# The down projection of two of four blocks as seven products of half-size matrices

## The chip, the cores and the metric

One core of one Trainium2 chip runs the whole step. The metric is the device time of one execution in microseconds, given as the median of some runs; the profile is of one execution.

## The reference, cut to what matters

One layer of a streaming encoder on 2048 prompt frames and 32 frames of a running stream. All is float32.

```python
m = g[:, :, 0] * attn + g[:, :, 1] * conv
x = x + rmsnorm(m @ w_out, g_post_mix)
h = rmsnorm(x, g_pre_ffn)
f = (silu(h @ w_ffn_gate) * (h @ w_ffn_up)) @ w_ffn_down    # 1024 -> 2816 -> 1024
return x + rmsnorm(f, g_post_ffn)
```

The change touches the product with `w_ffn_down`: for 512 frames a matrix of 512 x 2816 times one of 2816 x 1024.

## The kernel before, in words

**Tiling.** The prompt is worked off in four blocks of 512 frames (`NB`, `T`); the last takes the 32 sample frames along (`ext(b)`). A block is a list of 80 steps (`KINDS`): 50 of input projection, attention and convolution, 8 of `w_out`, and 22 of `w_ffn_down` (from `S_D`); the gate and up stage stands between the last two. Each float32 product is made of three: an operand is split into a high part (rounded to fp32r, by ACT) and a low part (operand minus high part, by DVE), and PE computes high x high, high x low and low x high into one PSUM bank.

**Gate and up** (`gate_and_up`, L1406). Pairs of 2 x 2 half-size matrices are multiplied with seven products instead of eight, 146 slots (`SLOTS`), 12 matmuls of 256 columns a product. The weights come as raw tiles or, from block 1 on, as stored sums of tiles, and are split on chip by `high_weights` (ACT, L1792) and `low_weights` (DVE, L2422), up to five units ahead of PE (`AHEAD`). In block 0 POOL forms the sums (`summed_weights`, L1161). The outputs f, 22 tiles of 128 features by 512 frames, are written by `copies_out` (ACT, L1841) and `products_out` (DVE, L2450; L2481 is its last multiplication).

**Down** (`token_major`, L1451, and `down_tail`, L1492). A step takes two tiles of f (256 features) and half of the output columns. `staged_hi` (L1825) and `staged_lo` (L2431) split f two tiles at a time, one step ahead. The weights, split in block 0 and stored in DRAM, come back as high and low tiles of 512 KB by `load_hi` and `load_lo` (L984, L997). For each of four frame tiles (128 frames) and each of the two feature tiles PE makes three matmuls of 512 columns (L1447 to L1449): the piece of f is the stationary operand, the weight streams. The results stand in all eight PSUM banks; the first two banks are copied out at half-time (`stash`).

**Beside the down stage** the next block's input norm is made, tile by tile in fixed steps (`s0_at`, L769): SP loads x (`load_x`), ACT sums squares (`sum_squares`, L1744), POOL takes the root (`inv_rms`, L1150), DVE scales (`scale_rows`, L2345), PE transposes (`transpose_tile`, L1289), DVE multiplies by the gains (`gains_in`, L2354), ACT rounds (`normed_hi`, L1786), DVE subtracts (`normed_lo`, L2363). After the last step each of four output tiles gets its root mean square (`post_squares`, `post_inv_rms`) and is added to x (`residual`, L2483); then SP stores y (`store_y`, L1047), and the next block's first convolution taps wait for that store.

**Order.** Every engine has its own queue, written out by hand, and works it off in order; semaphores (`w_used`: PE has used a step; `fhi_ok`, `flo_ok`: a piece of f is split; `hf_ok`, `hlo_ok`: a norm tile is made) tie them together. A wait in a queue holds all that stands behind it.

## Time and profile before

| | us |
|---|---|
| median of 3 runs | 2989.41 (2988.89 to 2991.73) |
| the profiled execution | 2988.57 |
| its span | 2986.8 |
| granted clock of TensorE, mean | 0.997 of 2.4 GHz |
| PE busy, share of the span | 98% |

The page gives, for one execution, the busy time of each engine (PE is TensorE, DVE VectorE, ACT ScalarE, POOL GpSimd, SP the engine that issues most DMAs), groups of instructions with their mean duration and what ended the idle time before them, and the DMAs. Matmuls overlap in their pipeline: their pace is read from start to start, not from the duration. The same holds, to a smaller degree, for ACT and DVE.

### The profile page before, as it was taken

How to read it: one execution, taken by the hardware profiler on the slowest of the kernel's cores; microseconds unless marked ns; L12 is line 12 of the kernel's file. 1: busy time of each engine (PE TensorE's matmuls, PEld its weight loads, DVE VectorE, ACT ScalarE, POOL GpSimd, SP SyncE). 2: the span in 40 equal slices, each digit the busy share in tenths (PEclk: the TensorE clock that was granted, in tenths of full speed). 3: DMA queues.
4: the chain of work that ended last, by engine and by line, in shares of the span. 5: the costliest groups of instructions: out<-in, count | busy, mean ns of one | idle time of the engine just before them, and what ended most of it. 6: DMA issues, size and time to landing. Idle time of an engine off the chain costs nothing. (4 is left out here: it accounts for less than half of the span.)

```text
span 2986.8 us, 50911 instructions
## 1 busy us (share of the span) xinstructions
PE 2932.4 (98%) x18791; PEld 2618.2 (88%) x18791; DVE 2030.7 (68%) x3674; ACT 1451.5 (49%) x2877; POOL 680.0 (23%) x658
## 2 busy tenths in 40 slices
PE   8999999999999999999999999999999999999998
PEld 7777789988888889998888888999899999899976
DVE  8998779874797747663398775665369867466623
ACT  5766555554455535553155544554225554455412
POOL 4950035520581000000086000000039400100001
PEclk9999999999999999999999999999999999999999
DMA  8875746678654355556655444556565443445543
GB/s 297 274 244 200 268 146 210 206 280 300 223 190 166 128 187 166 179 182 226 218 195 185 142 156 158 188 186 210 196 208 173 169 132 121 170 157 172 178 168 122
DMA packets 204454, 573.44 MB, mean 192 GB/s; under 512 B 24000, under 2 KB 26816, under 8 KB 203696
## 3 DMA queue, kind: packets, MB, share of 16 engines
q1 hardware_dynamic: 191728, 548.81, 54.2%
q10 hardware_dynamic: 12480, 21.38, 1.9%
q8 instruction: 151, 2.47, 0.3%
q14 instruction: 95, 0.78, 0.1%
HBM read 456.03 MB, written 114.16 MB: 191 GB/s over the span
## 5 line engine op out<-in xcount | busy, mean ns | idle before, releaser
L1325 PE MATMUL PS<-h_hi,w_hi 128*128 128x512 f32 (+2 forms) x1664 | 533.4, 353 | 9.0 <-DVE u L2710 5.4
L1325 PE MATMUL PS<-h_hi,w_lo 128*128 128x512 f32 (+2 forms) x1664 | 525.3, 349 | 0.0
L1325 PE MATMUL PS<-h_lo,w_hi 128*128 128x512 f32 (+2 forms) x1664 | 525.3, 348 | 0.0
L1355 PE MATMUL PS<-op_hi,w_hi 128*128 128x256 f32 x1680 | 476.6, 284 | 2.2 <-DVE w_lo L2429 2.2
L1355 PE MATMUL PS<-op_lo,w_hi 128*128 128x256 f32 x1680 | 475.4, 283 | 0.0
L1355 PE MATMUL PS<-op_hi,w_lo 128*128 128x256 f32 x1680 | 475.4, 283 | 0.0
L1221 POOL TENSOR_TENSOR y<-y,prod 128x512 f32<-128x512 f32 (+1 forms) x333 | 431.8, 1325 | 157.9 <-ACT prod L1947 144.9
L2314 DVE SCALAR_TENSOR_TENSOR PS<-u,dw,PS 128x512 f32<-128x512 f32 (+1 forms) x604 | 434.1, 766 | 7.0
L2429 DVE TENSOR_TENSOR w_lo<-raw,w_hi 128x512 fp32r<-128x512 f32 x376 | 287.8, 775 | 155.1 <-ACT w_hi L1799 154.3
L1325 PEld LDWEIGHTS PS<-h_hi,w_hi 128*128 128x128 f32 x1664 | 293.9, 188 | 53.3 <-issue 13.1
L1325 PEld LDWEIGHTS PS<-h_hi,w_lo 128*128 128x128 f32 x1664 | 294.0, 188 | 39.3
L1325 PEld LDWEIGHTS PS<-h_lo,w_hi 128*128 128x128 f32 x1664 | 294.3, 188 | 38.5 <-issue 1.4
L1355 PEld LDWEIGHTS PS<-op_hi,w_hi 128*128 128x128 f32 x1680 | 322.4, 192 | 4.0 <-DVE w_lo L2429 3.9
L1355 PEld LDWEIGHTS PS<-op_lo,w_hi 128*128 128x128 f32 x1680 | 322.5, 192 | 0.0
L1355 PEld LDWEIGHTS PS<-op_hi,w_lo 128*128 128x128 f32 x1680 | 322.5, 192 | 0.0
L1192 POOL TENSOR_TENSOR prs<-pss 128x1 f32<-128x1 f32 x34 | 9.3, 274 | 1315.8 <-ACT tmp L1899 1315.8
L1447 PE MATMUL PS<-w_hi,f_hi 128*128 128x512 f32 x704 | 275.4, 391 | 2.0 <-DVE f_lo L2439 1.3
L1947 ACT ACTIVATE prod<-u,dw 128x512 f32<-128x512 f32 (+1 forms) x333 | 234.7, 732 | 83.1 <-POOL y L1221 82.8
L1449 PE MATMUL PS<-w_hi,f_lo 128*128 128x512 f32 x704 | 274.4, 390 | 0.0
L1448 PE MATMUL PS<-w_lo,f_hi 128*128 128x512 f32 x704 | 274.4, 390 | 0.0
L1799 ACT ACTIVATE w_hi<-raw 128x512 fp32r<-128x512 f32 x376 | 225.2, 622 | 50.9 <-POOL raw L1184 50.9
L1833 ACT ACTIVATE f_hi<-f 128x1024 fp32r<-128x1024 f32 (+1 forms) x88 | 94.3, 1072 | 279.6 <-PE PS L1449 177.1
(316 smaller groups left out, 5864.0 us busy)
## 6 DMA issues: line engine op xcount, KB each, us to landing
w_lo<-lo_dram SPq DMA_DIRECT2D x240, 512.0 KB, 4.5
w_hi<-hi_dram SPq DMA_DIRECT2D x240, 512.0 KB, 3.6
raw<-in_w_stream SPq DMA_DIRECT2D x292, 256.0 KB, 3.4
w_raw<-sum_dram SPq DMA_DIRECT2D x180, 256.0 KB, 3.0
w_raw<-in_w_stream SPq DMA_DIRECT2D x80, 512.0 KB, 5.2
hi_dram<-w_hi SPq DMA_DIRECT2D x80, 512.0 KB, 5.6
lo_dram<-w_lo SPq DMA_DIRECT2D x80, 512.0 KB, 3.7
sum_dram<-raw ACTq DMA_DIRECT2D x60, 256.0 KB, 2.3
```

Of the source, the lines that this page charges most:

```text
L1192: link(nc.gpsimd.tensor_tensor(prs[:, c, :], pss[:, tt, 0:1], pss[:, tt, 1:2], ALU.add))
L1221: nc.gpsimd.tensor_tensor(y[:, ct, 0:yw], y[:, ct, 0:yw], prod[:, n % RING, 0:yw], ALU.add).then_inc(prod_used, 1)
L1325: last = nc.tensor.matmul(PS[:, k0 + off, col:col + n], w, x[:, k, c0:c0 + n], start=first and k == 0, stop=stop and k == KT - 1)
L1355: last = nc.tensor.matmul(out, w[:, part_k], o[:, k, :], start=start and first and k == 0, stop=stop and k == KH - 1, skip_group_check=again)
L1447: nc.tensor.matmul(out, hi, wk[0], start=first, stop=False)
L1448: nc.tensor.matmul(out, hi, wk[1], start=False, stop=False)
L1449: return nc.tensor.matmul(out, lo, wk[0], start=False, stop=last_k)
L1799: A(product_hi(m), source(b, m), ACT.Copy).then_inc(wh_ok, 1)
L1833: A(f_hi[:, dd % 2, :, 0:c], f[:, 2 * kp:2 * kp + 2, 0:c], ACT.Copy).then_inc(fhi_ok, 1)
L1947: A(prod[:, n % RING, 0:yw], u[:, ct, k:k + yw], ACT.Copy, scale=dw[:, ct, k:k + 1]).then_inc(prod_ok, 1)
L2314: ins = STT(out, src, dw[:, ct, k:k + 1], acc(b, ct), ALU.mult, ALU.add)
L2429: TT(product_lo(m), source(b, m), product_hi(m).bitcast(F32), ALU.subtract).then_inc(wl_ok, 1)
```

## The change

In blocks 1 and 2 (`SEVEN`) the down product is cut into a 2 x 2 scheme too: first and second half of the frames, even and odd tiles of f, first and second half of the output columns. Seven products, each of 256 frames by 11 tiles of 128 features by 512 columns, take the place of eight. A piece is one product's one feature tile: 77 pieces (`DOWN`), and in each two frame tiles and three matmuls, six matmuls of 512 columns of the same kind as before.

- The factors that are sums or differences of pieces of f are formed on POOL in place (`sum_of_pieces`, 44 of the 77 pieces), nine pieces ahead as its queue is written. ACT and DVE split each piece's factor, 128 x 256 (`high_piece`, `low_piece`), five pieces ahead, in a ring of six.
- The weights are no longer read back split: all seven come as raw tiles of 128 x 512 and are split by ACT and DVE in each of the two blocks. Products 1, 2 and 3 read the weight as it is; 4 to 7 read sums, which POOL forms during block 1's gate and up stage (`sums_of_weights`: 88 sums, 66 DMAs issued by POOL) and stores in `t_dram`. The room for this, `t_sum`, lies over f's last three tiles and a part of x's buffer, so ACT waits for the last store before it writes f's tile 19, and SP before it loads x.
- The products are combined by one copy each of ACT behind products 1, 6 and 7 (`hold`) and five additions of 128 x 1024 on DVE.
- The norm steps of the next block hang on pieces (`STEP_END`: step dd ends with piece 3, 6, 10, 13, 17, 20, 24, 27, 31 ...), and its PSUM pair is the same two banks for all four tiles, so a tile's squares wait for the gains of the one before.
- Squares and residuals of output tiles 0 and 1 move to pieces 70 and 74; those of tiles 2 and 3 stay at the end.

```diff
+SEVEN = (1, 2)
+MAKES_T = SEVEN[0]
+KEPT = ()
+X2, Z2, Y2, W2 = 2, 4, 6, 0
+def passes():
+    order = []
+    for lead, other in ((1, 5), (2, 6), (4, 7)):
+        order += [(lead, 0), (lead, 1)]
+        for e in range(HALF_D - 2):
+            order += [(lead, e + 2), (other, e)]
+        order += [(other, HALF_D - 2), (other, HALF_D - 1)]
+    return order + [(3, e) for e in range(HALF_D)]
+DOWN = passes()
+ND7 = len(DOWN)
+DSLOT = {ie: n for n, ie in enumerate(DOWN)}
+PLACE = [v % 7 if v < 49 else (v - 49) % 8 for v in range(ND7)]
+FR = 6
+DAHEAD = 5
+SUM_AHEAD = 9
+SUMS_F = [(i, e) for i in (5, 6, 7, 3) for e in range(HALF_D)]
+SUM_POS = {ie: n for n, ie in enumerate(SUMS_F)}
+STEP_END = [-(-7 * (dd + 1) // 2) - 1 for dd in range(FT)]
+W_USED_AT = {v: v - 1 for v in range(1, 18)} | {71: 17, 73: 18, 74: 19, 75: 20}
...
+        d_hi = at("d_hi", R_u, [P, FR, 2 * P], F32R)
+        d_lo = at("d_lo", R_u + FR * 2 * P * 4, [P, FR, 2 * P], F32R)
+        held = at("held", R_u + 2 * FR * 2 * P * 4, [P, 2, T])
+        third = at("third", R_u + 2 * FR * 2 * P * 4 + 2 * T * 4, [P, 2, T])
...
+        t_sum = at("t_sum", R_g + (FT - 3) * TX * 4, [P, 2, 2, 2, T // 2])
...
+        t_dram = nc.dram_tensor("t_dram", [HALF_D, 2, P, 2, 2, T // 2], F32, kind="Internal").ap()
...
+        def loaded_later(g):
+            return g >= NS and not (seven(g // NS) and g % NS >= S_D)
...
+        def turned_before(eng, b, tt):
+            if b and seven(b - 1):
+                if tt:
+                    eng.wait_ge(hf_ok, first_norm(b, tt))
+            elif b and tt >= 2:
+                eng.wait_ge(hf_ok, first_norm(b, tt) - 1)
...
+        def place_free(eng, b, v):
+            before = [u for u in range(v) if PLACE[u] == PLACE[v]]
+            if before:
+                down_used(eng, b, before[-1])
+            else:
+                unit_used(eng, b, NU - 8 + PLACE[v])
...
+            def down_units(b):
+                k = 0
+                for v, (i, e) in enumerate(DOWN):
+                    place_free(sp, b, v)
...
+                    elif i < 4:
+                        s = S_D + 2 * FT + e + (HALF_D if i == 3 else 0)
+                        cols_of = slice(0, HW) if i == 1 else slice(HW, 2 * HW)
+                        sp.dma_start(down_raw(v), w_stream[s, :, cols_of]).then_inc(rawq_in[PLACE[v]], 16)
+                    else:
+                        half, odd = {5: (0, 0), 4: (0, 1), 7: (1, 0), 6: (1, 1)}[i]
+                        sp.dma_start(down_raw(v).rearrange("p (c n) -> p c n", c=2),
+                                     t_dram[e, :, :, half, odd, :].rearrange("c p n -> p c n")
+                                     ).then_inc(rawq_in[PLACE[v]], 16)
+                    for dd in steps_at(v - DAHEAD):
+                        if dd % 2 and (dd + 1) // 2 < tiles(b + 1):
+                            load_x(b + 1, (dd + 1) // 2)
...
+            def sums_of_weights():
+                pool.wait_ge(op_ok, len(OPS) * (MAKES_T + 1))
+                made = len(SUMS) * NP
+                for e in range(HALF_D):
+                    for n in range(2):
+                        if e == 0:
+                            load_of_sums(e, n)
+                        elif n == 0:
+                            load_of_sums(e, 0)
+                            load_of_sums(e, 1)
+                    for n in range(2):
+                        b11, b21, b12, b22 = (t_sum[:, n, half, odd, :] for half in range(2) for odd in range(2))
+                        pool.wait_ge(t_in[n], 32 * (e + 1))
+                        nc.gpsimd.tensor_tensor(b11, b12, b11, ALU.subtract).then_inc(ws_ok, 1)
+                        pool.wait_ge(ws_ok, made + 1)
+                        nc.gpsimd.tensor_tensor(b12, b22, b12, ALU.subtract).then_inc(ws_ok, 1)
+                        pool.wait_ge(ws_ok, made + 2)
+                        nc.gpsimd.tensor_tensor(b22, b22, b11, ALU.subtract).then_inc(ws_ok, 1)
+                        pool.wait_ge(ws_ok, made + 3)
+                        nc.gpsimd.tensor_tensor(b21, b21, b22, ALU.subtract).then_inc(ws_ok, 1)
+                        made += 4
+                        pool.wait_ge(ws_ok, made)
+                        pool.dma_start(t_dram[e, n], t_sum[:, n]).then_inc(t_out[n], 16)
+            def load_of_sums(e, n):
+                if e:
+                    pool.wait_ge(t_out[n], 16 * e)
+                cols_of = slice(n * T // 2, (n + 1) * T // 2)
+                for half in range(2):
+                    src = w_stream[S_D + 2 * FT + half * HALF_D + e].rearrange("p (k n) -> p k n", k=2)
+                    pool.dma_start(t_sum[:, n, half], src[:, :, cols_of]).then_inc(t_in[n], 16)
...
+            def sum_of_pieces(b, i, e):
+                a11, a12, a21, a22 = first_half(e, 0), first_half(e, 1), second_half(e, 0), second_half(e, 1)
+                if i == 5:
+                    up_out(pool, b, e)
+                    out, one, other, op = a21, a21, a22, ALU.add
+                elif i == 6:
+                    low_piece_made(pool, b, DSLOT[1, e])
+                    sum_made(pool, b, (5, e))
+                    out, one, other, op = a11, a21, a11, ALU.subtract
+                elif i == 7:
+                    low_piece_made(pool, b, DSLOT[5, e])
+                    sum_made(pool, b, (6, e))
+                    out, one, other, op = a21, a22, a11, ALU.subtract
+                else:
+                    low_piece_made(pool, b, DSLOT[2, e])
+                    sum_made(pool, b, (6, e))
+                    out, one, other, op = a12, a12, a11, ALU.subtract
+                nc.gpsimd.tensor_tensor(out, one, other, op).then_inc(ws_ok, 1)
+            def sums_for(b, first, end):
+                for v in range(first, min(end, ND7)):
+                    if DOWN[v] in SUM_POS:
+                        sum_of_pieces(b, *DOWN[v])
...
+                        if b == MAKES_T:
+                            sums_of_weights()
+                    if s == S_D and seven(b):
+                        sums_for(b, 0, SUM_AHEAD)
+                        for v in range(ND7):
+                            sums_for(b, v + SUM_AHEAD, v + SUM_AHEAD + 1)
+                            for dd in steps_at(v):
+                                start, _, _ = s0_at(S_D + dd, b)
+                                if start is not None:
+                                    inv_rms(b + 1, start, 0)
...
+            def down_of_seven(b):
+                for v, (i, e) in enumerate(DOWN):
+                    if i in KEPT:
+                        down_landed(pe, b, v)
+                    else:
+                        pe.wait_ge(weight_low_ok, 1 + raw_units(b, v))
+                    low_piece_made(pe, b, v)
+                    k = {1: X2, 6: X2, 7: X2, 5: Z2, 2: Y2, 3: Y2, 4: W2}[i]
+                    if e == 0:
+                        if i in (1, 5, 2):
+                            for bank in (k, k + 1):
+                                out_made(pe, b, *last_read(bank))
+                        elif i == 4:
+                            pe.wait_ge(hf_ok, first_norm(b + 1, tiles(b + 1) - 1) + 1)
+                        elif i == 3:
+                            combined(pe, b, 1)
+                        else:
+                            pe.wait_ge(copies_ok, 1 + 3 * sevens_before(b) + (1 if i == 6 else 2))
+                    hi, lo = down_high(v), down_low(v)
+                    for t in range(2):
+                        x_hi, x_lo = (d[:, v % FR, t * P:(t + 1) * P] for d in (d_hi, d_lo))
+                        for x, w, start, stop in ((x_hi, hi, True, False), (x_hi, lo, False, False),
+                                                  (x_lo, hi, False, True)):
+                            last = nc.tensor.matmul(PS[:, k + t, :], x, w, start=start and e == 0 and i not in (6, 7),
+                                                    stop=stop and e == HALF_D - 1, skip_group_check=i in (6, 7))
+                        if t == 0 and v in W_USED_AT:
+                            last.then_inc(w_used, 1)
+                    last.then_inc(w_used if v == ND7 - 1 else dm_used, 1)
+                    for dd in steps_at(v):
+                        _, trans, _ = s0_at(S_D + dd, b)
+                        if trans is not None:
+                            transpose_tile(b + 1, trans, 0)
...
+            def high_piece(b, v):
+                if v >= ND7:
+                    return
+                i, e = DOWN[v]
+                if v < FR:
+                    finished(act, b, (FT - 1, 2))
+                else:
+                    down_used(act, b, v - FR)
+                if (i, e) in SUM_POS:
+                    sum_made(act, b, (i, e))
+                elif i in (1, 4):
+                    up_out(act, b, e)
+                A(d_hi[:, v % FR, :], f_piece(v), ACT.Copy).then_inc(fhi_ok, 1)
+                if i not in KEPT:
+                    down_landed(act, b, v)
+                    place_free(act, b, v)
+                    A(down_high(v), down_raw(v), ACT.Copy).then_inc(weight_high_ok, 1)
+            def hold(b, v):
+                down_used(act, b, v)
+                if DOWN[v][0] == 1:
+                    out = stash_of(b, 1)
+                else:
+                    out = held[:] if DOWN[v][0] == 6 else third[:]
+                    finished(act, b, (FT - 1, 4))
+                A(out, two_banks(X2), ACT.Copy).then_inc(copies_ok, 1)
+            def down_of_seven(b):
+                for v, (i, e) in enumerate(DOWN):
+                    high_piece(b, v + DAHEAD)
+                    if i in (1, 6, 7) and e == HALF_D - 1:
+                        hold(b, v)
+                    for dd in steps_at(v):
+                        start, _, out = s0_at(S_D + dd, b)
+                        if out is not None:
+                            normed_hi(b + 1, out)
+                        if start is not None:
+                            sum_squares(b + 1, start, 0)
+                    if v == DSLOT[3, 4]:
+                        combined(act, b, 4)
+                        first_squares(b, 1)
+                        post_squares(b, 0, 1)
+                        post_squares(b, 1, 1)
...
+                    if b == MAKES_T and j == FT - 3:
+                        for n in range(2):
+                            act.wait_ge(t_out[n], 16 * HALF_D)
...
+                            if LAST_SLOT - 7 <= slot < LAST_SLOT - 7 + DAHEAD and seven(b):
+                                high_piece(b, slot - LAST_SLOT + 7)
...
+                if seven(b):
+                    combined(act, b, 5)
+                    post_squares(b, 2, 1)
+                    post_squares(b, 3, 1)
...
+            def low_piece(b, v):
+                if v >= ND7:
+                    return
+                dve.wait_ge(fhi_ok, pieces_before(b) + v + 1)
+                TT(d_lo[:, v % FR, :], f_piece(v), d_hi[:, v % FR, :].bitcast(F32), ALU.subtract).then_inc(flo_ok, 1)
+                if DOWN[v][0] not in KEPT:
+                    dve.wait_ge(weight_high_ok, 1 + raw_units(b, v))
+                    TT(down_low(v), down_raw(v), down_high(v).bitcast(F32), ALU.subtract).then_inc(weight_low_ok, 1)
+            def down_of_seven(b):
+                for v, (i, e) in enumerate(DOWN):
+                    low_piece(b, v + DAHEAD)
+                    if e == HALF_D - 1:
+                        if i == 2:
+                            down_used(dve, b, v)
+                            dve.wait_ge(copies_ok, 1 + 3 * sevens_before(b) + 1)
+                            TT(stash_of(b, 1), two_banks(Y2), stash_of(b, 1), ALU.add).then_inc(c_ok, 1)
+                        elif i == 6:
+                            dve.wait_ge(copies_ok, 1 + 3 * sevens_before(b) + 2)
+                            TT(held[:], two_banks(Z2), held[:], ALU.add).then_inc(c_ok, 1)
+                        elif i == 7:
+                            dve.wait_ge(copies_ok, 1 + 3 * sevens_before(b) + 3)
+                            combined(dve, b, 2)
+                            TT(two_banks(Z2), two_banks(Z2), third[:], ALU.add).then_inc(c_ok, 1)
+                            combined(dve, b, 3)
+                            TT(third[:], two_banks(W2), third[:], ALU.add).then_inc(c_ok, 1)
+                        elif i == 3:
+                            down_used(dve, b, v)
+                            TT(held[:], two_banks(Y2), held[:], ALU.add).then_inc(c_ok, 1)
+                    for dd in steps_at(v):
+                        start, _, out = s0_at(S_D + dd, b)
+                        if out is not None:
+                            gains_in(b + 1, out)
+                        if start is not None:
+                            scale_rows(b + 1, start)
+                        if out is not None:
+                            normed_lo(b + 1, out)
+                    if v == DSLOT[3, 8]:
+                        residual(b, 0, 1)
+                        residual(b, 1, 1)
...
+                            if LAST_SLOT - 6 <= slot < LAST_SLOT - 6 + DAHEAD and seven(b):
+                                low_piece(b, slot - LAST_SLOT + 6)
...
-                for tt in range(4):
+                for tt in range(2 if seven(b) else 0, 4):
...
```

Not shown: counts of semaphores that follow from the new number of pieces, and four semaphores renamed.

## Rows read from the trace of the kernel before

**Rows 1.** The page: its span, and busy time of the engines.

```profile
span 2986.8 us, 50911 instructions
...
PE 2932.4 (98%) x18791; PEld 2618.2 (88%) x18791; DVE 2030.7 (68%) x3674; ACT 1451.5 (49%) x2877; POOL 680.0 (23%) x658
```

**Rows 2.** Windows: stretch, us, busy PE, PEld, DVE, ACT, POOL, clock, DMA share, GB/s.

```profile
390.00:626.00 236.00, 230.33 (x1872) 227.28 (x1872) 201.91 (x265) 127.49 (x269) 119.65 (x92) 0.99 0.54 185
1106.00:1341.00 235.00, 233.08 (x1903) 230.64 (x1902) 157.23 (x267) 130.64 (x274) 5.74 (x17) 1.00 0.52 164
1346.50:1470.00 123.50, 123.50 (x562) 102.38 (x561) 43.21 (x46) 36.09 (x49) 6.46 (x17) 1.00 0.59 202
```

**Rows 3.** Timeline, PE, block 1 down stage; columns: start us, us, instruction.

```profile
1346.54 0.40 PE L1447 MATMUL PS<-w_hi,f_hi 128*128 128x512 f32 x1
...
1357.22 0.39 PE L1449 MATMUL PS<-w_hi,f_lo 128*128 128x512 f32 x1
...
1357.45 1.03 PE L1302 MATMUL PS<-ident_sb,xs 128*128 128x128 f32 x8
...
1470.01 0.39 PE L1325 MATMUL PS<-h_hi,w_hi 128*128 128x512 f32 x1
```

**Rows 4.** Timeline of block 0 gate and up stage: DVE, then ACT.

```profile
499.89 0.41 DVE L2463 TENSOR_TENSOR part<-PS,part 128x256 f32<-128x256 f32 x1
...
500.22 0.68 DVE L2429 TENSOR_TENSOR w_lo<-s_sum,w_hi 128x512 fp32r<-128x512 f32 x1
...
500.82 0.41 DVE L2457 TENSOR_TENSOR f<-PS,f 128x256 f32<-128x256 f32 x1
...
502.25 0.62 ACT L1799 ACTIVATE w_hi<-raw 128x512 fp32r<-128x512 f32 x1
...
502.77 0.41 ACT L1856 ACTIVATE f<-f 128x256 f32<-128x256 f32 x1
```

**Rows 5.** The page, DMA issues; last column: median us from issue to landing.

```profile
w_lo<-lo_dram SPq DMA_DIRECT2D x240, 512.0 KB, 4.5
...
raw<-in_w_stream SPq DMA_DIRECT2D x292, 256.0 KB, 3.4
```

**Rows 6.** Timeline, DVE, norms of the next block in block 1 down stage.

```profile
1360.01 1.28 DVE L2360 TENSOR_TENSOR xs<-PS,gn 128x512 f32<-128x512 f32 x2
...
1364.37 0.75 DVE L2350 TENSOR_SCALAR xs<-xs,stats 128x1024 f32<-128x1024 f32 x1 [3.08 <-POOL stats L1158]
...
1366.18 1.22 DVE L2439 TENSOR_TENSOR f_lo<-f,f_hi 128x1024 fp32r<-128x1024 f32 x1
...
1397.74 1.22 DVE L2366 TENSOR_TENSOR h_lo<-xs,h_hi 128x1024 fp32r<-128x1024 f32 x1 [1.13 <-ACT h_hi L1789]
```

**Rows 7.** Block 0 against block 1 for L2481; timeline of a clash; POOL sum L1230.

```profile
L2481 DVE TENSOR_TENSOR f<-f,part x18: 1506/1510/1515, 445.0 to 618.6; 128x256 f32<-128x256 f32 x18
...
L2481 DVE TENSOR_TENSOR f<-f,part x19: 415/419/420, 1160.8 to 1341.4; 128x256 f32<-128x256 f32 x19
...
504.07 1.56 POOL L1184 TENSOR_TENSOR raw<-raw,raw 128x512 f32<-128x512 f32 x1
...
504.74 1.44 DVE L2429 TENSOR_TENSOR w_lo<-raw,w_hi 128x512 fp32r<-128x512 f32 x1
...
L1230 POOL TENSOR_TENSOR sq_sum<-y x4: 1286/1295/1432, 181.8 to 2337.0; 128x512 f32<-128x512 f32 x3, 128x574 f32<-128x574 f32 x1
```

**Rows 8.** Waits of PE in block 0; last operand and tile 19 of block 1.

```profile
PE PS L1355 <- DVE w_lo L2429: 2.2, 4, 1.4
...
1149.19 1.23 DVE L2418 TENSOR_TENSOR op_lo<-h,op_hi 128x1024 fp32r<-128x1024 f32 x1
...
1313.62 0.38 ACT L1847 ACTIVATE f<-PS 128x256 f32<-128x256 f32 x1 [0.54 <-PE PS L1355]
```

**Rows 9.** Timeline, DVE then PE, mean of y in block 2.

```profile
1615.06 0.69 DVE L2328 TENSOR_TENSOR sq_sum<-sq_sum,rest_sum 128x512 f32<-128x512 f32 x1
...
1618.85 1.02 PE L1616 MATMUL PS<-sq_sum,ones 128*128 128x512 f32 x2
```

156 lines of the change are left out of this document (123 added, 33 removed).

## The prediction

> **What bounds the kernel now.** I read the page's table of engines, then windows by stage, then the timelines. The page: PE is busy for 98% of the span, DVE for 68% [rows 1]. The windows: in block 1's gate and up stage PE is busy 233 of 235 us and DVE 157; in its down stage PE 123.5 of 123.5 and DVE 43 [rows 2]. So a down stage lasts as long as its matmuls, and fewer of them shorten it as long as the others can feed PE at the new pace. The median of the runs, 2989.4, lies 0.8 above the profiled execution's 2988.6, whose span is 2986.8; I add differences to the median. About 0.2% (6 us) is what can be told from no change.
>
> **What goes.** A matmul of 512 columns is shown as 0.39 us long, but the next starts 0.227 us later (1357.22 to 1357.45) [rows 3]. A stage has 22 steps x 4 token tiles x 2 x 3 = 528 of them, 119.7 us. It runs from 1346.54 to 1470.01, 123.5 us; the other 3.8 are four groups of eight transposes with the seams around them, 0.95 a group. Afterwards a stage has 77 pieces x 2 x 3 = 462 matmuls, 104.7 us (1.36 a piece), and with the 3.8 108.5. Alone that is 15.0 a stage, 30.0 in two.
>
> **What each piece costs the others.** Counted from start to start, DVE takes 0.60 us for 512 columns and 0.33 for 256; ACT takes 0.52 for 512 and at most 0.41 for 256 [rows 4]. DVE now makes the low half of a factor (256) and of a weight (512): 0.93 us a piece; ACT 0.93 at most. Both are under 1.36. The first five pieces are made in the last slots of the gate and up stage, where DVE waits on PE anyway. The weights' DMAs (256 KB each 1.36 us, 193 GB/s, against 202 now [rows 2]) delay nothing of themselves, since a place is refilled seven pieces ahead (9.5 us) and a load lands in 3.4 [rows 5]. But they set where DVE is: the weight of piece v+5 is asked for when v-2 is done and lands 3.5 later, then come ACT (0.55) and DVE (0.7), so DVE reaches what stands behind low_piece(v+5) some 3.4 us after PE starts v.
>
> **The norms of the next block** stand in DVE's queue there. One in the middle runs so now [rows 6]: gains_in at 1360.01, ACT's copy and squares, POOL's root, scale_rows at 1364.37, normed_lo, next instruction at 1366.18. That is 6.17 us of DVE's queue, 3.08 of it waiting, and 5.1 to the scaled tile. The last has no scaling: 1.28 + 1.13 of waiting + 1.22 = 3.6. In the new order they stand at pieces 10, 17, 24 and 31, and PE's transposes of the tile scaled at 10 stand behind piece 13, 5.4 us after the start of 10. The tile is ready at 3.4 + 5.1 = 8.5: PE waits 3.1. From norm to norm DVE needs 6.17 + 7 x 0.93 = 12.7; round the loop (5.1 to the tile, 0.95, three pieces 4.1, 3.4 to the next norm) it is 13.5. PE's own work is 10.5.
>
> **POOL's sums** are the term that decides. 44 of the 77 pieces need a sum on POOL, of two SBUF tensors of 256 columns. Where POOL adds, DVE instructions with two SBUF inputs stand still: L2481 (256 columns) takes 1510 ns in block 0, all 18 times, and 419 in block 1; in the timeline a w_lo issued under a POOL sum ends 0.55 after it, and that sum itself is 0.27 longer than its usual 1.29 [rows 7]. Both DVE instructions of a piece have two SBUF inputs. POOL needs 1.29 for 512 columns and 1.43 for 574 [rows 7], so for 256 about 0.72, an estimate. Of POOL's 1.29 DVE lost 1.09; of 0.72 it then loses 0.52. The ends: nothing (the sums fall into DVE's waits) and the whole 0.72. I take 0.52, since DVE has no slack where the sums lie. POOL's queue is tied to the pieces only through inv_rms: after 10 it makes three sums, after 17 four, and after 24 nothing holds it, so the last 28 come as fast as it can make them, two a piece, some 25 of them under DVE's work.
>
> The Trainium skill (GPSIMD Engine Reference, Specifications) says the same of the SBUF interfaces: "contention with DVE instructions in a 2-port perf mode or with two SBUF inputs"; the trace agrees with it (1510 ns against 419). The same page (Instruction dispatch) gives about 2.5 cycles an element for a two-input loop, at its 1.2 GHz 0.53 us for 256 columns; by that estimate a sum costs DVE 0.33, and two stages come out 12 us shorter than below. For 512 columns it would give 1.07 where the rows have 1.29, so the rows stand.
>
> **One stage**, from the start of piece 10 to that of 42: 3.4, then 12.7 + 3 x 0.52 = 14.3, then 12.7 + 4 x 0.52 = 14.8, then 6.17 + 13 x 0.93 + 3.6 + 25 x 0.52 = 34.9; together 67.4. PE alone needs 32 x 1.36 + 3 x 0.95 = 46.4 and so stands 21.0. The stage takes 108.5 + 21.0 = 129.5 instead of 123.5: 6.0 more, 12.0 in two. Behind 42 DVE (0.93) is faster than PE again and no sums are left; the additions that combine the products wait for PE with five pieces (6.8 us) in hand, and ACT's `hold` copies have the same cover.
>
> **Block 1's gate and up stage** gets 88 sums and 66 DMAs on POOL. (a) DVE goes from 157 us busy to 157 + 88 x 0.52 = 203 of 235, what block 0 has (202), and there PE waited 2.2 for w_lo [rows 2, 8]. I take 2; ends 0 and 5. (b) No DMA issued by POOL is in the trace. A round has two transfers one behind the other (3.5 each, by the nearest rows [rows 5]) and eight sums with their gaps (6.8), each 0.27 late behind DVE as in [rows 7] (2.2): 16.0, eleven rounds 176. The last operand is made at 1150.4, and ACT writes f's tile 19 at 1313.6 [rows 8], 163 later. Its wait then holds ACT 13 us; weights are split five ahead (7 us), so PE stands 6. Ends: 0 (rounds under 14.8) and 30 (rounds of 18.2). The Trainium skill (DMA: Bandwidth & Descriptors, Specifications) has about 1 us to the first byte for DMAs issued by GpSimd against 0.6 for the others; that would add 0.8 a round, 9 in all, to (b), and no run here shows it. SP waits for the same stores before the next x and the first piece, hidden if ACT's wait is.
>
> **Elsewhere.** (c) load_x(2) holds SP until the first normed_lo; the load of piece 19 comes about 3 us late, inside the 14.3. (d) Two of four tiles' squares and residuals move into the stage. The other two come behind an addition of 1.2; the last residual ends some 8.6 after the last matmul, now 5.8, and the store of y, and the first tap after it, as much later. y's mean is ready at 1615.75 and PE uses it at 1618.85 [rows 9]: 3.1 of cover for 2.8. 0; without cover up to 3 a boundary. (e) `w_used` opens the next block's first weights 4.5 pieces (6.1 us) before the end; a 512 KB load lands in 4.5 [rows 5]. 0; ends 0 and 2.
>
> Total: 2989.4 + 12.0 + 2 + 6 = 3009.
>
> **Rivals.**
> *No clash, the norms bind (faster).* POOL's sums fall where DVE waits. From 10 to 42: 3.4 + 13.5 + 13.5 + 25.1 (5.1 + 0.95 + 14 x 1.36) = 55.5; PE stands 9.1, stage 117.6, two save 11.8: 2978. It decides if a sum costs DVE less than about 0.2. For it: block 0's 80 sums cost DVE 45 us (202 against 157), 0.56 each for twice the columns, and PE 2 [rows 2, 8]. Against: there DVE had slack and read PSUM often. 0.15.
> *All hidden.* The lead of five pieces covers norms and sums: 2989.4 - 30.0 = 2959. The place of the transposes speaks against it. 0.07.
> *Half a clash.* 0.3 a sum: 32 x 0.22 = 7.0 less a stage: 2989.4 - 2.0 + 3 = 2990. 0.13.
> *Whole sums lost, or late stores.* 0.72: 32 x 0.20 = 6.4 more a stage, 3009 + 13 = 3022; or (b) at its end, 3009 + 24 = 3033. 0.20.
> *It doesn't do what it says*: that PE's count does not fall is excluded by the loops, 77 x 6 against 528.
> Forecast 0.45, from 2997 to 3018.
>
> **How the numbers follow.** Faster by over 0.2%: 0.15 + 0.07 = 0.22. Within: 0.13. Slower: 0.45 + 0.20 = 0.65. The range leaves out the hidden case (0.07) and the upper half of the late stores: 2972 to 3028.
>
> **What would show it.** Pieces 1.36 apart until 10; PE waiting on DVE's xs before the second to fourth group of transposes, 2 to 4 us each; w_lo stretched to 1.2 us, with PE waiting on it, between pieces 28 and 42, under 28 POOL sums in a row; then none; stages of 129. In block 1, ACT waiting for a store of t_dram at tile 19. Wrong if w_lo keeps its 0.69 there, if PE's waits sit behind 42 (then a DMA or `hold`), or if POOL's sums of weights are done long before 1313.

## The result, and the profile after

The changed kernel takes 3044.9 us (3041.9 to 3048.6, 4 runs) against 2990.6 (2988.9 to 2994.4, 4 runs): ratio 1.018, interval 1.0163 to 1.0198. It is 54 us slower where 20 were forecast, above the forecast's 2997 to 3018 and above the wider range's 3028. The profiled execution is the slowest of the four (3048.6); its span is 60.0 us longer than that of the profiled execution before, and the places below are counted in it.

The page, as in [rows 1]:

```profile
span 3046.8 us, 51830 instructions
...
PE 2925.1 (96%) x18659; PEld 2606.4 (86%) x18659; DVE 2189.2 (72%) x3948; ACT 1547.6 (51%) x3143; POOL 899.5 (30%) x900
```

The windows of block 1's gate and up stage, the part of it in which POOL works, and the two down stages, as in [rows 2] (busy time of PE, PEld, DVE, ACT, POOL, then clock, DMA share, GB/s):

```profile
1119.00:1375.30 256.30, 229.66 (x1890) 229.09 (x1890) 176.41 (x273) 129.11 (x274) 129.83 (x164) 0.95 0.74 245
1150.00:1316.00 166.00, 166.00 (x1386) 166.00 (x1385) 128.80 (x199) 91.55 (x200) 106.51 (x128) 1.00 0.90 301
...
1375.30:1510.60 135.30, 117.69 (x497) 94.25 (x496) 110.66 (x174) 80.43 (x172) 46.23 (x53) 0.94 0.53 162
2102.30:2238.10 135.80, 116.80 (x504) 93.87 (x503) 110.87 (x178) 82.26 (x175) 49.87 (x55) 0.96 0.53 162
```

PE has less to do than before and still the span is longer. From first matmul to first matmul, in us:

| part | before | after | more |
|---|---|---|---|
| start to block 1's gate and up | 1119.0 | 1120.3 | 1.3 |
| block 1's gate and up | 227.5 | 255.0 | 27.5 |
| its down stage | 123.5 | 135.3 | 11.8 |
| to block 2's gate and up | 362.6 | 364.2 | 1.6 |
| block 2's gate and up | 227.6 | 227.5 | -0.1 |
| its down stage | 124.4 | 135.8 | 11.4 |
| to block 3's gate and up | 407.3 | 412.7 | 5.4 |
| the rest | 395.0 | 396.0 | 1.0 |

Who made PE wait, over the whole span (us in total, times, longest):

```profile
PE PS L1564 <- DVE xs L2712: 26.5, 7, 5.7
PE PS L1617 <- ACT f L2198: 24.7, 1, 24.7
PE PS L1798 <- DVE w_lo L2812: 10.1, 12, 4.1
...
PE PS L1587 <- DVE x L2916: 5.2, 1, 5.2
```

None of the four stood before. Each row is read: who waited, for whose result, us in total, times, longest. L1564 are the transposes of the next norm and `xs` the scaled tile that they take; L1617 are the gate and up products, L1798 the seven down products with `w_lo` the low half of their weight, L1587 block 3's first steps.

**The wait at tile 19.** From the timelines, one round of POOL, and ACT behind the last store (start us, us, instruction; in brackets the idle time before it and what ended it):

```profile
1278.48 1.45 POOL L1419 DMA_DIRECT2D t_sum<-in_w_stream  x2 [0.16 <-issue]
1282.15 1.42 POOL L1419 DMA_DIRECT2D t_sum<-in_w_stream  x2 [2.22 <-DMA t_dram<-t_sum]
1285.76 0.73 POOL L1401 TENSOR_TENSOR t_sum<-t_sum 128x256 f32<-128x256 f32 x1 [2.20 <-DMA t_sum<-in_w_stream]
1286.57 0.74 POOL L1403 TENSOR_TENSOR t_sum<-t_sum 128x256 f32<-128x256 f32 x1
1287.39 1.07 POOL L1405 TENSOR_TENSOR t_sum<-t_sum 128x256 f32<-128x256 f32 x1
...
1296.03 1.45 POOL L1419 DMA_DIRECT2D t_sum<-in_w_stream  x2
...
1343.39 0.38 ACT L2198 ACTIVATE f<-PS 128x256 f32<-128x256 f32 x1 [29.00 <-DMA t_dram<-t_sum]
```

7.3 us pass from the issue to the first sum and 10.3 with eight sums (0.73 alone, 1.07 beside DVE) and two issues of stores: 17.6 for this round. In this stretch (1150 to 1360) loads issued by POOL land in 5.9 us (median), its stores in 4.2. From 1152.0 to 1343.4 are eleven rounds, 191. PE stands 24.7 of the 27.5; the other 2.8 are matmuls at the lower clock behind it (granted clock 0.53 over 1344 to 1350).

**The down stage** of block 1. The timeline of DVE behind the norm after which nothing holds POOL:

```profile
1430.72 1.21 DVE L2712 TENSOR_SCALAR xs<-xs,stats 128x1024 f32<-128x1024 f32 x1 [3.08 <-POOL stats L1347]
...
1434.38 1.21 DVE L2812 TENSOR_TENSOR w_lo<-w_raw,w_hi 128x512 fp32r<-128x512 f32 x1
1435.52 0.96 DVE L2809 TENSOR_TENSOR d_lo<-f,d_hi 128x256 fp32r<-128x256 f32 x1
1436.40 1.22 DVE L2812 TENSOR_TENSOR w_lo<-w_raw,w_hi 128x512 fp32r<-128x512 f32 x1
1437.55 0.96 DVE L2809 TENSOR_TENSOR d_lo<-f,d_hi 128x256 fp32r<-128x256 f32 x1
```

POOL's timeline beside it (27 sums in one row):

```profile
1430.65 27.47 POOL L1439 TENSOR_TENSOR f<-f 128x256 f32<-128x256 f32 x27
```

In block 2 the same burst comes later, since block 3 has a fifth norm tile; and PE waits for `w_lo` under it (POOL, then PE):

```profile
2171.29 28.03 POOL L1439 TENSOR_TENSOR f<-f 128x256 f32<-128x256 f32 x25
...
2188.43 0.50 PE L1798 MATMUL PS<-w_hi,d_hi 128*128 128x512 f32 x1 [1.02 <-DVE w_lo L2812]
```

PE's timeline in block 1 at three of its waits and behind the second:

```profile
1398.87 1.09 PE L1564 MATMUL PS<-ident_sb,xs 128*128 128x128 f32 x8 [3.16 <-DVE xs L2712]
1415.94 1.97 PE L1564 MATMUL PS<-ident_sb,xs 128*128 128x128 f32 x8 [5.71 <-DVE xs L2712]
...
1418.14 0.63 PE L1798 MATMUL PS<-w_lo,d_hi 128*128 128x512 f32 x1
1418.57 0.63 PE L1798 MATMUL PS<-w_hi,d_lo 128*128 128x512 f32 x1
...
1453.55 0.79 PE L1798 MATMUL PS<-w_hi,d_hi 128*128 128x512 f32 x1 [4.10 <-DVE w_lo L2812]
```

Two stretches behind the second and the third wait shown, with the granted clock third from the end:

```profile
1418.00:1424.00 6.00, 6.00 (x21) 4.72 (x21) 4.88 (x10) 1.77 (x5) 1.02 (x2) 0.72 0.76 236
1454.00:1460.00 6.00, 6.00 (x17) 4.63 (x17) 6.00 (x8) 2.86 (x7) 5.24 (x6) 0.59 0.15 44
```

And whom SP's queue waited for with its loads of x, in this stage:

```profile
SPq L1060 <- DVE h_lo L2728: 17.5, 2, 10.4
```

Under 27 POOL sums in a row a piece takes DVE 2.03 us (1435.52 to 1437.55) instead of 0.93, 0.55 a sum. Behind the wait of 5.7 us two matmuls stand 0.43 apart, not 0.227, and the transposes take 1.97 instead of 1.09: the granted clock is 0.72 over 1418 to 1424, that is 1.2 GHz for a part of it and 2.4 for the rest. SP stood 10.4 and 7.1 us with a load of x, and the next weights were behind it.

**Between blocks 2 and 3**, DVE's timeline up to the last residual:

```profile
2234.40 0.42 DVE L2809 TENSOR_TENSOR d_lo<-f,d_hi 128x256 fp32r<-128x256 f32 x1 [2.80 <-ACT d_hi L2149]
...
2240.85 1.22 DVE L2834 TENSOR_TENSOR held<-PS,held 128x1024 f32<-128x1024 f32 x1
...
2248.75 0.69 DVE L2916 TENSOR_TENSOR x<-x,held 128x512 f32<-128x512 f32 x1
```

PE's, behind it:

```profile
2249.49 0.82 PE L1587 MATMUL PS<-h_hi,w_hi 128*128 128x256 f32 x2 [5.21 <-DVE x L2916]
```

The next block's first matmul starts at 2238.13, so the stage's matmuls are over; the last addition could start then and starts at 2240.85, and the last residual ends at 2249.4, 11.3 later.

### The profile page after: what moved, and what is told of

Read it like the earlier page. It is cut to its first block and busy times, and to the rows that moved or that the text cites. A ratio compares the mean times of both kernels' runs of the same rounds, so it can differ in the third digit from the quotient of the medians.

```text
span 3046.8 us, 51830 instructions
## 1 busy us (share of the span) xinstructions
PE 2925.1 (96%) x18659; PEld 2606.4 (86%) x18659; DVE 2189.2 (72%) x3948; ACT 1547.6 (51%) x3143; POOL 899.5 (30%) x900
## 5 line engine op out<-in xcount | busy, mean ns | idle before, releaser
L1587 PE MATMUL PS<-h_hi,w_hi 128*128 128x512 f32 (+2 forms) x1664 | 534.7, 354 | 12.6 <-DVE x L2916 5.2
L1587 PE MATMUL PS<-h_lo,w_hi 128*128 128x512 f32 (+2 forms) x1664 | 527.1, 350 | 0.0
L1587 PE MATMUL PS<-h_hi,w_lo 128*128 128x512 f32 (+2 forms) x1664 | 527.0, 350 | 0.0
L1617 PE MATMUL PS<-op_hi,w_hi 128*128 128x256 f32 x1680 | 479.3, 285 | 28.3 <-ACT f L2198 24.7
L1617 PE MATMUL PS<-op_lo,w_hi 128*128 128x256 f32 x1680 | 477.2, 284 | 0.0
L1617 PE MATMUL PS<-op_hi,w_lo 128*128 128x256 f32 x1680 | 477.1, 284 | 0.0
L1617 PEld LDWEIGHTS PS<-op_hi,w_hi 128*128 128x128 f32 x1680 | 324.3, 193 | 31.0 <-issue 24.9
L1587 PEld LDWEIGHTS PS<-h_hi,w_hi 128*128 128x128 f32 x1664 | 295.8, 189 | 56.3 <-issue 10.6
L1587 PEld LDWEIGHTS PS<-h_hi,w_lo 128*128 128x128 f32 x1664 | 295.6, 189 | 39.3
L1587 PEld LDWEIGHTS PS<-h_lo,w_hi 128*128 128x128 f32 x1664 | 295.8, 189 | 38.8 <-issue 1.4
L1617 PEld LDWEIGHTS PS<-op_lo,w_hi 128*128 128x128 f32 x1680 | 324.4, 193 | 0.0
L1617 PEld LDWEIGHTS PS<-op_hi,w_lo 128*128 128x128 f32 x1680 | 324.3, 193 | 0.0
L2791 DVE TENSOR_TENSOR w_lo<-w_raw,w_hi 128x512 fp32r<-128x512 f32 x180 | 132.2, 734 | 62.7 <-ACT w_hi L2100 58.0
L1617 PE MATMUL PS<-op_hix,w_lo 128*128 128x288 f32 (+1 forms) x560 | 162.5, 290 | 0.0
L1617 PE MATMUL PS<-op_lox,w_hi 128*128 128x288 f32 (+1 forms) x560 | 162.0, 289 | 0.0
L1617 PE MATMUL PS<-op_hix,w_hi 128*128 128x288 f32 (+1 forms) x560 | 161.9, 289 | 0.0
```

The costliest lines, as they stand in the source:

```text
L1587: last = nc.tensor.matmul(PS[:, k0 + off, col:col + n], w, x[:, k, c0:c0 + n], start=first and k == 0, stop=stop and k == KT - 1)
L1617: last = nc.tensor.matmul(out, w[:, part_k], o[:, k, :], start=start and first and k == 0, stop=stop and k == KH - 1, skip_group_check=again)
L2791: TT(product_lo(m), source(b, m), product_hi(m).bitcast(F32), ALU.subtract).then_inc(wl_ok, 1)
```

## The experiments

Where nothing else is said a kernel was run once, beside one run of the kernel before (2988 to 2990), so small differences of totals tell nothing. Block 1's wait at tile 19 varied in the seven kernels that keep it and the whole weight sums (16.8 to 24.7 us), so the stages are compared, not only totals. The expectations take differences read in the profiled execution (3048.6) off the median (3045), which makes them up to 3.7 too low. A stage pair such as 135.3 / 135.8 is block 1's and block 2's down stage.

### Which engine's work it is: the sums of pieces on one column

```diff
-nc.gpsimd.tensor_tensor(out, one, other, op)
+nc.gpsimd.tensor_tensor(out[:, 0:1], one[:, 0:1], other[:, 0:1], op)   # in sum_of_pieces
```


> Leaves out: the 44 sums of pieces of f in each of the two stages are made on one column instead of 256 (the products 5, 6, 7, 3 are then fed wrong factors); all waits, splits and matmuls stay. Theory 1 (POOL's sums stop DVE, 0.5 us each, and the stops lengthen PE's waits and drop its clock): d_lo and w_lo keep 0.41 and 0.68 us everywhere, PE's waits for w_lo (5.9 and 4.2 us) go, the waits for xs shrink from 11.7 and 14.7 to about 8 to 10, and the stages fall from 135.3 and 135.8 us to 118 to 125; total 3045 less 20 to 34: 3011 to 3025. Rival (the norms' chain alone sets the stage, the sums fall in its gaps): stages stay at 130 or more, total 3035 or more.

3018.9, of which 8 come from a shorter wait at tile 19 (16.8). Stages 124.2 / 127.1 (the second 2 above what was expected), with the same 174 to 178 DVE instructions, now 92.49 us instead of 110.66:

```profile
1366.90:1491.10 124.20, 113.80 (x497) 93.38 (x496) 92.49 (x175) 80.21 (x172) 22.35 (x53) 0.96 0.57 177
```

(Columns as above; block 1's stage.) So the 44 sums cost DVE 18 us a stage, 0.41 each, and PE 11 and 9. PE's waits for `w_lo` go (5.9 to 0.5 in block 1); those for `xs` stay nearly as long (9.9 and 13.5).

### The weight sums, two ways

On one column, with their DMAs whole:

```diff
-nc.gpsimd.tensor_tensor(b11, b12, b11, ALU.subtract)
+nc.gpsimd.tensor_tensor(b11[:, 0:1], b12[:, 0:1], b11[:, 0:1], ALU.subtract)   # all four
```


> Leaves out: the 88 sums of weights in block 1 are made on one column instead of 256 (products 4 to 7 then read wrong weights); their 66 DMAs stay whole. Theory 1 (a round of 17.4 us is 8.6 of POOL's additions under DVE plus the two transfers and POOL's own issue): a round takes 11 to 13 us, all stored by 1295, ACT's wait at tile 19 and PE's 24.7 us behind it are gone, total 3045 less 27 to 30: about 3016. Rival (the DMAs are the round, since the 16 DMA engines are 90% busy there): rounds stay above 15 us and PE still waits 5 us or more there, total above 3022.

3023.3. A round takes 13.1 (1183.95 to 1196.99), the gate and up stage 227.7 against 227.5 before: nothing of the DMAs reaches PE, although their share is 0.93. The total was expected at about 3016 and lies where the rival had it (above 3022), but what the rival says, rounds above 15 and a wait that stays, is not there. 3.7 of the difference is the base of the forecast, and 2.4 was lost before block 1's gate and up.

With their buffer over the two x buffers, so that ACT waits for nothing:

```diff
-t_sum = at("t_sum", R_g + (FT - 3) * TX * 4, [P, 2, 2, 2, T // 2])
+t_sum = [at("t_sum0", R_g + FT * TX * 4, [P, 2, 2, T // 2]), at("t_sum1", R_qs, [P, 2, 2, T // 2])]
...
-                    if b == MAKES_T and j == FT - 3:      # ACT, copies_out
-                        for n in range(2):
-                            act.wait_ge(t_out[n], 16 * HALF_D)
...
+                    if v == X_AT:                         # SP, down_units; X_AT = 6
+                        if b == MAKES_T:
+                            for n in range(2):
+                                sp.wait_ge(t_out[n], 16 * HALF_D)
+                        load_x(b + 1, 0)
```
(Not shown: SP also waits for each sum's own store before it reads it.)

> Same sums, same DMAs, but their buffer lies over the two x buffers instead of f's last three tiles: ACT has nothing to wait for, and SP waits for each piece's own store, and for the last one only before it loads x (now ahead of piece 6's weight). Theory 1: the stores end at 1343 as before, the stage starts at about 1347 instead of 1375.3, the lost clock comes back too, and the total is 3045 less 28: 3017, between 3014 and 3021. Rival (the wait only moves: SP stands for the last store and piece 6 and x come late, so PE stands in the first ten pieces instead): 3025 to 3040.

3026.8: by its total the rival's (3025 to 3040), by its places the theory's. The gate and up stage takes 231.9: 23 of the 27.5 are back, and no wait has moved into the first ten pieces. 3.1 of the other 4.4 is a new wait between 1347 and 1351 (the waits of PE):

```profile
PE PS L1622 <- DVE part L2870: 3.1, 1, 3.1
```

There the last sums of weights and the first five sums of pieces run in one go beside DVE. The stage behind it is as before (135.1 / 136.3).

### The norm steps wider apart, then the standing taken out

```diff
-STEP_END = [-(-7 * (dd + 1) // 2) - 1 for dd in range(FT)]
+STEP_END = [2, 6, 9, 15, 17, 23, 25, 31, 33, 38, 40] + [40 + dd for dd in range(11, FT)]
```


> The norm steps of the next block lie wider apart: starts behind pieces 2, 9, 17, 25, 33, transposes behind 6, 15, 23, 31, 38, instead of starts behind 3, 10, 17, 24, 31 and transposes behind 6, 13, 20, 27. Theory 1 (PE waits for xs because three pieces are too short for a loop of DVE, ACT and POOL): the waits for xs (11.7 and 14.7 us) fall under 3 each, with them most of the clock lost to them; the waits for w_lo stay or shrink since the last burst of POOL sums is shorter; stages 122 to 128 us, total 3045 less 15 to 27: 3018 to 3030. Rival (DVE has no time left in the stage, so what is won at xs is lost at w_lo): stages stay above 131, total above 3036.

3035.0, stages 132.2 / 132.9. The rival was nearer: the waits for `xs` before the transposes are gone (0 and 0.5; in block 2 one of 2.6 for a tile's gains is new), and those for `w_lo` grew from 5.9 and 4.2 to 14.7 and 12.0.

```diff
+                            low_piece_made(pool, b, v)          # POOL, ahead of the sum for piece v + 9
...
-                            scale_rows(b + 1, start)            # DVE, at v
+                            scale_rows(b + 1, start)            # at v + 2; normed_lo at v + 1
```


> The wide norm steps, and with them: DVE scales a tile's rows two pieces behind its gains instead of at once (it splits two pieces in the 3.1 us in which it waited for ACT and POOL), subtracts one piece behind; and POOL makes the sum for piece v+9 only when DVE has split piece v, so there is no burst of 25 sums. Theory (the stage is DVE's: 110 us of instructions, of which POOL's sums are some 17, plus 12 us of standing for ACT and POOL per stage): the standing goes, the sums stay; stages fall from 132 to 120 to 126, total 3045 less 22 to 35: 3010 to 3023. Rival (the burst and the standing were not what held DVE; it waits for weights or for ACT): stages stay above 129.

3026.9, stages 123.7 / 128.6: the total and the second stage lie above their ranges. DVE's busy time is the same (110.1 / 112.7), so what went is standing. Two edits act here together, the order and the pacing of the sums, and were not told apart. But it now stands up to 2.5 us for ACT's split, which ACT holds behind its own wait for the gains.

### SP's hold alone

```diff
-                    for dd in steps_at(v - DAHEAD):         # SP, down_units
+                    for dd in steps_at(v - DAHEAD - 2):
```


> The changed kernel, with one edit: SP's load of the next x tile stands two pieces later in its queue (before the weight of piece 22 instead of 20, and so on). In the changed kernel SP waits there for the subtraction of the tile two before, 10.4 and 7.1 us in block 1's down stage, with the next weights behind it. Theory A (this hold is a link of the loop: weights come late, DVE stands for ACT and ACT for the DMA, the norm comes late): the waits for xs fall by 3 us or more in a stage, stages from 135.3 and 135.8 to 128 to 132. Theory B (the hold only fills slack, seven places ahead, as the prediction took it): stages within 1.5 us of before.

3038.8, stages 131.6 / 133.7, 3.7 and 2.1 less: the direction of theory A, but less than it asked for (block 2's stage is above its 132, and the waits for `xs` fell by 2.7 and 2.0, from 11.7 to 9.0 and from 14.7 to 12.7). SP's hold itself was halved, from 17.5 to 8.4.

### Matmuls in the place of waits

```diff
+                    if any(s0_at(S_D + dd, b)[1] for dd in steps_at(v)):
+                        for _ in range(10):
+                            last = nc.tensor.matmul(PS[:, k + 1, :], x_lo, hi, start=False, stop=False, ...)
```


> Adds to the changed kernel ten matmuls of 512 columns (2.3 us at 0.227) to each piece behind which the second to last tile is transposed, three in block 1's down stage and four in block 2's, in the place where PE now waits 3 to 6 us for xs; they add a product into the open sum, so the output is not the layer's. Theory (a wait of PE over some 4 us is followed by matmuls at 1.2 GHz, and that is 9 us of each stage on top of the waits): the waits for xs fall from 11.7 and 14.7 by about 2.3 each time, the transposes take 1.09 instead of 1.97 us, and although there are 30 and 40 more matmuls the stages get shorter by 2 to 5 us. Rival (the low clock has nothing to do with these waits, or costs nothing): stages the same within 1 us, or up to 7 us longer.

3037.5, stages 134.0 / 135.1. 30 and 40 more matmuls (6.8 and 9.1 us at 0.227) cost nothing, which the waits account for only in part: these fell by 5.4 and 6.9. Beyond its matmuls and waits a stage took 6.6 and 4.6 us where it took 9.3 and 7.5. The direction is the theory's, its size (2 to 5 us shorter) was not reached, and kernels with the same stage differ by up to 1.5 us (133.8 to 135.3), so the stages alone are support and no proof. The traces settle more of it. In the changed kernel the granted clock is at its lower level for 17.1 us of block 1's stage and 10.2 of block 2's, and the 41 and 31 matmuls and transposes that start in these stretches lose 6.5 and 4.5 us against their usual pace from start to start. In the filler run the stretches are 10.2 and 3.4 us long and the loss is 4.0 and 1.5. So nearly all of what the rest fell by (2.7 and 2.9) is the lower clock. The Trainium skill (TensorE: Matmul & The Clock Gate, Part 1) has the array at 1.2 GHz after idling and at 2.4 when it has been busy; the rows at 1415.94 agree with it.

### The boundary of blocks 2 and 3

```diff
                     if s == 1 and ext(b):
-                        pe.wait_ge(pn_ok, post_tile(b - 1, 3, 1) + 1)
+                        pe.wait_ge(copies_ok, 1 + 3 * sevens_before(b))
```


> The changed kernel, but PE's second step of block 3 no longer waits for the last residual of block 2: the banks that it writes were last read by ACT's copy of product 7, and it waits for that. Theory (the 5.2 us that PE stands there for x, and the slow matmuls after it, are this wait, over the last residual that now ends 11.3 us after the last matmul, before 6.0): the wait goes, part of it comes back two steps on, where u needs the same residual; from the end of block 2's down stage to the next gate stage 412.7 us become 408 to 410, total 3045 less 3 to 5, though 3 us either way is what block 1's wait for the stores varies. Rival: u needs the residual just as much, and the wait only moves to DVE u: 412 or more.

3030.2; from the end of the stage to block 3's gate and up 408.7 instead of 412.7, of which 1.9 is a wait for u. (Most of the rest of its gain is a shorter wait at tile 19, 17.1.)

### All of it together

Buffer over x, wide steps, paced sums, and at the end of a stage ACT's first squares at piece 68 and DVE's first residual at 71:

> The kernel of the run before, with the weight sums' buffer over the x buffers (no wait of ACT at tile 19) and, at the end of a stage, ACT's squares of the first two output tiles two pieces earlier and DVE's residual of the first tile three pieces earlier. Theory: 20 us less from the buffer as measured, 3 to 5 us less from the boundary of blocks 2 and 3 (PE's wait of 5.2 us for x falls under 2): 2985 to 3000. Rival: the earlier residuals take DVE time it does not have in the last pieces, and the gain of the boundary is lost in the stage: 3000 or more.

3006.6, the rival's total; stages 124.1 / 129.8, and PE's wait for x still 5.3: the earlier residuals gave nothing. With product 1's weights read back split (`KEPT = (1,)`):

> As the run before, but product 1's weights (11 of 77 pieces) come back split from DRAM, as in the kernel before: DVE and ACT each do 11 instructions of 512 columns less in the first 22 pieces, 6.6 and 5.7 us, and the DMAs move 2.8 MB more. Theory (DVE bounds the stage): 4 to 7 us less a stage than the run before, 8 to 14 in all. Rival (the DMAs, or something later in the stage, bind): within 2 us of the run before, or slower.

3006.9: the rival. DVE had 7 us less (103.3) in block 1 and the stage was no shorter (124.7); PE's waits for `xs` were 7.9 there, so the norm chain held it. Then, from the kernel at 3006.6, the order of the chain, together with the edit of the boundary run above:

```diff
-                    for dd in steps_at(v):                      # ACT: normed_hi, sum_squares
+                    for dd in steps_at(v - 1):                  # sum_squares, behind high_piece(v + 5)
+                    for dd in steps_at(v - 2):                  # normed_hi
...
+                    for dd in steps_at(v - 1):                  # DVE: scale_rows; normed_lo at v - 2
```


> As the run with buffer, wide norms, paced sums and earlier ends, with the wait of the run above taken off, and another order of a norm step: ACT splits piece v+6 first, then squares the next tile, and rounds the finished tile a piece later; DVE splits piece v+6 behind the gains, then scales, and subtracts a piece later. Theory (PE's 9 and 13 us of waits for xs in that run are ACT and DVE waiting for each other in turn: DVE 2.5 us for a split that ACT holds behind its wait for the gains, ACT 3.9 us for the gains): the tile is scaled some 3.5 us sooner, the waits for xs fall under 4 in a stage, the stages from 124 and 130 to 116 to 121; total 3007 less 17 to 25: 2982 to 2990. Rival (DVE's 110 us of instructions bind now): stages stay above 122, and the waits are for w_lo.

2992.5, stages 120.7 / 125.4, total and second stage above what the theory gave; waits for `xs` before the transposes 1.6 and 3.5, and one of 2.9 for the gains in block 2. The same with `KEPT = (1,)`:

> The same with product 1's weights read back split. Theory: with the norm steps out of the way DVE is next, so its 6.6 us less a stage now show: 2 to 6 us less a stage than the run before. Rival: norm steps still bind, equal within 2 us.

2989.9, stages 119.9 / 125.7: the stages within 2 again. What ACT waited for in block 1's stage points to the next link, weights that come late behind SP's hold:

```profile
ACT w_hi L2162 <- DMA w_raw<-t_dram: 26.0, 18, 4.8
```

In the kernel with all weights raw (2992.5) this wait was 16.7. From that kernel SP's loads of x went two pieces later and the steps to `[1, 6, 8, 14, 16, 22, 24, 30, 31, 36, 38]`:

> The kernel with the new order of a norm step, all weights raw, with the loads of x two pieces later and all norm steps one or two pieces earlier (last gains behind piece 38, before 40). Theory A: ACT no longer waits 26 us in a stage for weights of the sums (4.8 us the longest); stages from 120.7 and 125.4 to 115 to 118; 2992 less 8 to 14: 2978 to 2984. Theory B: 2990 or more.

2979.4, stages 116.9 / 122.1 (the second above its range); ACT waits 7.0 there instead of 16.7. Which of the two edits gave how much was not told apart. The same with `KEPT = (1,)`:

> The same with product 1's weights read back split. If DVE's instructions (109 to 112 us of a stage with all weights raw, 104 to 107 with these) are now the bound: 3 to 6 us less a stage than the run before. If the matmuls are (108.5 us): within 2 us.

2978.3, stages 116.9 / 121.1: no shorter stage in block 1, 1.0 in block 2. Its DVE time is saved in the first 22 pieces, and PE's waits stand at pieces 23, 24, 31, 32, 71 and 74 with and without it; only one of 0.4 lay earlier. So this is no sign that the matmuls bind (the last run has them at 108.4). The kernel at 2979.4 once more, in more runs:

> The kernel of the run at 2979.4 once more, timed in five rounds against the kernel before. Theory: 2977 to 2982, 0.2 to 0.4% faster than before, outside the interval. Rival: the single run was a good one, and the two kernels differ by less than 0.1%.

2986.0 (11 runs) against 2990.5 (15 runs), ratio 0.9988, interval 0.9979 to 0.9997. The one run at 2979.4 was a good one: 2986.0 lies above the range that was expected, and the kernel is 0.12% faster than before, which the interval just tells from nothing. It is clearly faster than the changed kernel, and barely faster than the one before.

And this kernel with the sums of pieces of f on one column:

> The same kernel with the sums of pieces of f made on one column (products 5, 6, 7 and 3 get wrong factors). What is left of the clash: DVE has 108 and 111 us of instructions in stages of 116.9 and 122.1, of which the trace before and the run with narrow sums put 16 to 18 on POOL's stops. Theory: PE's waits for w_lo (4.5 and 6.0 us, all just behind a norm) go and the stages fall to 110 to 113; total less 12 to 18: 2962 to 2968. Rival: the waits come from the norm steps alone, less than 5 us less.

2961.0 in one run, 25 below the median of the mended kernel and 21.1 below its profiled execution (2982.1), more than expected; the stages are 8.9 and 12.2 shorter, which is all of the 21.1. The window of block 1's down stage, of the mended kernel:

```profile
1345.60:1462.90 117.30, 112.73 (x496) 88.54 (x495) 108.23 (x174) 80.24 (x173) 60.78 (x54) 1.00 0.63 192
```

And with the sums on one column:

```profile
1348.40:1456.80 108.40, 108.40 (x496) 89.90 (x495) 93.21 (x176) 80.80 (x172) 23.12 (x54) 1.00 0.67 205
```

Without the sums' time no wait of PE is left in the stages, and they are 108.4 / 109.4, the second with a fifth group of transposes. So taking POOL's sums off DVE's time is enough to bring the mended stage down to its matmuls. Waits shown make up only half of the 8.9: 4.6 us of them in block 1 and 4.3 beside them, at a granted clock of 1.00. A matmul is shown 0.39 us long where the next can start 0.227 after it, so each wait is some 0.16 longer than it is shown, and delays under 0.16 show as none.

## Why the prediction was right or wrong

**Right: the matmuls.** 108.5 a stage was taken; 108.4 was measured when nothing else bound (109.4 in block 2, whose fifth norm tile the prediction left out). That is 15 us a stage, but in a kernel whose sums leave out all but one column; with whole sums no run came under 116.9 and 121.1.

**Right: the waits in the stage, and in block 1 their places.** 21.0 us of standing were worked out from piece 10 to 42; the profile has 17.6 and 18.9. By its terms some 11 stood before the transposes and 10 under the burst of sums; block 1 has 11.7, at the second to fourth transposes (2.9 to 5.7 each), and 5.9 under 27 sums in a row, at pieces up to 37, and none behind. In block 2 the fifth norm tile moves the burst: 14.7 stand before four groups of transposes, and 4.2 at pieces 44 to 49. By the prediction's own sign, a wait behind 42 pointed to a DMA or `hold`; here it is `w_lo` under the sums. The sum on POOL was estimated at 0.72 and is 0.72. Its price to DVE, 0.52, is 0.55 in the burst and 0.41 over the stage. The Trainium skill (SBUF — State Buffer, Terms) says of the port pair of DVE and GpSimd that "the loser fully blocks"; the trace has both lengthened, each sum from 0.72 to 1.02 and DVE by 0.55. Laid end to end two sums and one piece would take 2.37 (2 x 0.72 + 0.93) where the row has 2.03, so for most of the time the two stand for each other, but not for all of it.

**Wrong: "The stage takes 108.5 + 21.0".** The sum has only matmuls at full pace and waits. 108.4 + 17.6 are 126.0, the stage took 135.3; in block 2 109.4 + 18.9 are 128.3 against 135.8. The missing term is 9.3 and 7.5: slow matmuls behind the waits (0.43 apart, clock means 0.94 and 0.96), and what stopping and starting costs beside the wait shown. [rows 3] show a PE that never stops, so nothing of it could be read there, but it should have been bounded: most waits of some us have a price after them. With it the two stages give 23.2 more than before where 12.0 were forecast: 11.2 of the miss. Counted matmul by matmul in the trace, the lower clock is 6.5 of the 9.3 and 4.5 of the 7.5; 1.6 and 1.8 are the 0.16 by which each wait is shown too short, and the rest is mostly the first matmul behind a wait at full clock, behind which the next starts 0.31 to 0.34 later instead of 0.227. The narrow run has the same term: its stages are 124.2 and 127.1 where the rival *No clash* had 117.6, with 10.4 and 13.5 of waits against 9.1.

**Wrong in size: "(b) A round ... 16.0, eleven rounds 176 ... so PE stands 6".** The mechanism, its place and its waiting instruction were as forecast. A round took 17.4 on the average: 7.3 to the first sum (7.0 taken) and 10.3 for sums and issues (9.0 taken, without POOL's own time for its DMAs: 1.45 for a pair of loads, 0.57 for a store). Eleven times 1.4 are 15.4, and ACT's wait became 29.0 instead of 13. Of PE's cover 4.3 us were left, not 7. The step had rounds of 18.2 for 30 us as its end, and this end was nearer to the 24.7; taken as a point inside a range of 0 to 30 where PE loses a microsecond for each beyond 1313, it carried the largest error: 27.5 against 8 with (a), 19.5 of the miss. (a), taken at 2 with 5 as its end, cost nothing that can be seen in this kernel, since the wait and the slow matmuls behind it fill the 27.5; with the sums whole and no wait behind them the stage lost 4.4, in the narrow run 0.2.

**Wrong: "(d) ... cover 3.1: 0 (up to 3 a boundary)".** 1.6 and 5.4 were lost. The last residual ends 11.3 behind the last matmul, not 8.6, since ACT's bunch of squares at piece 70 holds the last split by 2.8 and DVE's two residuals then stand ahead of the last addition. And y's mean is not the first to need it: block 3's second step waits for the last residual by an inherited wait, for banks that the new stage no longer uses for it.

**Wrong, but small in its effect: "(c) ... about 3 us late, inside the 14.3".** SP is held 10.4 and 7.1 us; halving that gave 3.7 and 2.1 a stage. In the mended order ACT waited up to 4.8 us at a time for weights behind it; there the loads were moved together with the norm steps, so the share of each is open.

The rival "whole sums lost, or late stores" with its second half, 3033, came nearest; no case had late stores and slow matmuls together.

The rest of the 60.0 (2.2) lies before the change and at the end, within what these parts vary from run to run (block 1's gate and up began between 1114.6 and 1124.2 in kernels with the same code ahead of it).

## What to carry to other kernels

When a stage goes from bound by matmuls to bound by waits, add a second term to the waits for what PE loses behind and beside them; here 7 to 9 us on 18, of which 4.5 to 6.5 were the lower clock. A wait for the end of a long chain on another engine is safer costed at its late end: here eleven rounds, each 1.4 us longer than taken, used up the cover and then went to PE one for one. Or the room is found elsewhere, as here over the x buffers, and the wait is gone. An engine's queue in which a split for PE stands behind a norm's wait is mended first by order: ACT, DVE and SP each held the loop in turn, and less work on DVE in pieces where nothing waited for it (`KEPT`) gave next to nothing. Once the order was right, DVE's time was what was left, and the sums' share of it was worth 21 us.
